# Placing the tiles that TensorE reads at multiples of 1024 bytes in a two-layer decoder trunk

## The reference

```python
def swiglu_ffn(x, norm_pre, w_gate, w_up, w_down, norm_post):
    h = rms_norm(x, norm_pre)
    a = jax.nn.silu(jnp.einsum('bsd,df->bsf', h, w_gate)) * jnp.einsum('bsd,df->bsf', h, w_up)
    y = jnp.einsum('bsf,fd->bsd', a, w_down)
    return x + rms_norm(y, norm_post)
def reference(x, ...):
    for layer in range(DEPTH):
        if layer % 2 == 0:
            x = ab_layer(x, ...)
        else:
            x = conformer_conv_layer(x, ...)
        x = swiglu_ffn(x, ...)
    return x
```

## The kernel before, in words

| tile | before | remainder | after | remainder |
|---|---|---|---|---|
| x | 16,512 | 128 | 18,432 | 0 |
| xT_hi, xT_lo | 32,896, 49,280 | 128 | 34,816, 51,200 | 0 |
| raw, w_hi, w_lo | 65,664, 82,048, 98,432 | 128 | 67,584, 83,968, 100,352 | 0 |
| gpost, tok | 114,816, 123,008 | 128 | 116,736, 124,928 | 0 |
| ident, ones | 133,856, 134,400 | 736, 256 | 17,120, 17,632 | 736, 224 |
| mix_hi, cT_hi, hT_hi | 136,160 | 992 | 136,192 | 0 |
| mix_lo, cT_lo; hT_lo | 152,544; 181,216 | 992 | 152,576; 181,248 | 0 |
| vd_hi, vd_lo, c_hi, c_lo | 177,120 to 209,888 | 992 | 177,152 to 209,920 | 0 |
| g_now, g_tail | 187,552, 189,856 | 160, 416 | 187,584, 189,888 | 192, 448 |
| sig, lin, sq, prod, conv_sum | 194,432 to 210,816 | 896 | 194,464 to 210,848 | 928 |
| diag, bias_rows, ones_r | 215,040, 217,088, 225,280 | 0 | 215,072, 217,120, 225,312 | 32 |

## Time and profile before

### The profile page before, as it was taken

The page is one execution under the profiler, slowest core; times in us unless marked ns, Lnnn a source line. Parts: engine busy times, 40 slices in busy tenths (PEclk is TensorE's granted clock), DMA queues, the critical chain, the costliest instruction groups (busy, mean ns, idle before and its releaser), DMA issues.

```text
span 2093.9 us, 28886 instructions
## 1 busy us (share of the span) xinstructions
PE 2056.2 (98%) x10074; PEld 1727.1 (82%) x10074; DVE 1181.5 (56%) x1449; ACT 986.2 (47%) x1165; POOL 197.5 (9%) x118
## 2 busy tenths in 40 slices
PE   8999999999999999999999989999999999999998
PEld 6798888888888888888899967788888888888886
DVE  5745465555555544444599996565555555544444
ACT  5544464545455443433744475454444444443433
POOL 0000000000000000000688640000000000000000
PEclk9999999999999999999999989999999999999999
DMA  7735465555555555555455415465555555555554
GB/s 240 246 129 187 171 211 192 185 189 188 190 189 190 188 185 188 187 186 190 130 190 184 156 61 171 161 220 189 189 190 188 190 189 190 188 184 190 185 187 141
DMA packets 105128, 382.31 MB, mean 183 GB/s; under 512 B 11682, under 2 KB 12066, under 8 KB 104546
## 3 DMA queue, kind: packets, MB, share of 16 engines
q1 hardware_dynamic: 103968, 375.58, 53.9%
q0 software_dynamic: 944, 5.51, 0.8%
q10 hardware_dynamic: 148, 0.27, 0.0%
HBM read 379.21 MB, written 2.10 MB: 182 GB/s over the span
## 4 chain that ended last, share of the span: by engine, by line
PE 86%; DVE 8%; issue 3%; DMA 1%; ACT 1%; DVEq 0%; POOL 0%; SPq 0%; ACTq 0%; POOLq 0%
PE acc L1158 80%; DVE acc L1065 5%; PE acc L1169 1%; PE acc L1171 1%; PE acc L1170 1%; PE acc L1350 1%; DMA raw<-in_units 1%; DVE taps_now L1046 1%; PE acc L1208 0%; PE acc L1210 0%; ACT w_hi L458 0%; DVE w_lo L780 0%; DMA vecs<-in_vecs 0%; ACT junk L468 0%; DVE conv L1067 0%
## 5 line engine op out<-in xcount | busy, mean ns | idle before, releaser
L780 DVE SCALAR_TENSOR_TENSOR w_lo<-raw,vecs,w_hi 128x1024 fp32r<-128x1024 f32 x400 | 512.6, 1284 | 476.3 <-ACT w_hi L458 474.6
L458 ACT ACTIVATE w_hi<-raw,vecs 128x1024 fp32r<-128x1024 f32 x400 | 459.2, 1151 | 527.8 <-PE acc L1158 492.2
L458 ACT ACTIVATE w_hi<-raw 128x1024 fp32r<-128x1024 f32 x304 | 322.1, 1062 | 481.0 <-PE acc L1158 378.8
L778 DVE TENSOR_TENSOR w_lo<-raw,w_hi 128x1024 fp32r<-128x1024 f32 x236 | 288.9, 1225 | 345.6 <-ACT w_hi L458 345.6
L1158 PE MATMUL acc<-w_hi,xT_hi 128*128 128x512 f32 x1536 | 477.8, 392 | 6.1 <-DVE w_lo L780 5.5
L1158 PE MATMUL acc<-w_lo,xT_hi 128*128 128x512 f32 x1536 | 473.6, 390 | 0.0
L1158 PE MATMUL acc<-w_hi,xT_lo 128*128 128x512 f32 x1536 | 473.4, 389 | 0.0
L1158 PEld LDWEIGHTS acc<-w_hi,xT_hi 128*128 128x128 f32 x1536 | 285.3, 188 | 68.1 <-DVE w_lo L780 6.3
L1158 PEld LDWEIGHTS acc<-w_lo,xT_hi 128*128 128x128 f32 x1536 | 288.6, 188 | 60.5
L1158 PEld LDWEIGHTS acc<-w_hi,xT_lo 128*128 128x128 f32 x1536 | 288.6, 188 | 60.3
L1158 PE MATMUL acc<-w_hi,hT_hi 128*128 128x512 f32 x704 | 222.8, 397 | 0.0
(11 more groups left out here) (155 smaller groups left out, 1510.6 us busy)
## 6 DMA issues: line engine op xcount, KB each, us to landing
raw<-in_units SPq DMA_DIRECT2D x708, 512.0 KB, 3.3
gpost<-in_post POOLq DMA_DIRECT2D x4, 1024.0 KB, 5.8
x<-in_x SPq DMA_DIRECT2D x4, 512.0 KB, 8.6
out<-x SPq DMA_DIRECT2D x8, 256.0 KB, 2.8
tok<-in_lng POOLq DMA_DIRECT2D x1, 512.0 KB, 7.0
tok<-in_lnb POOLq DMA_DIRECT2D x1, 512.0 KB, 9.8
bs<-in_bs POOLq DMA_DIRECT2D x1, 256.0 KB, 7.3
taps<-in_taps ACTq DMA_DIRECT2D x1, 248.0 KB, 2.6
```

The costliest lines, as they stand in the source:

```text
L458: nc.scalar.activation(out, raw[:, s, :], ACT.Copy, scale=scale).then_inc(hi_ready, 1)
L778: ins = nc.vector.tensor_tensor(out[:, s, :], raw[:, s, :], hi[:, s, :], ALU.subtract)
L780: ins = nc.vector.scalar_tensor_tensor(out[:, s, :], raw[:, s, :], vecs[:, gain:gain + 1], hi[:, s, :], ALU.mult, ALU.subtract)
```

## The change

The order of the allocations is changed and a start alignment is asked for. The small tiles (`vecs`, `ident`, `ones`, `warm`, the sums and variances) are allocated first, and the large common ones (`x`, `xT_hi`, `xT_lo`, `raw`, `w_hi`, `w_lo`, `gpost`, `tok`, `junk`, `rs_row`) behind them, each at a multiple of 1024 bytes. Of the stages' tiles, `mix_*`, `vm`, `vd_*`, `c_*`, `bs`, `cT_*`, `conv` and `hT_*` also get multiples of 1024. No instruction, wait, loop or DMA is added, removed or moved.

```diff
--- before.py
+++ after.py
@@ -40,6 +40,7 @@
 TAPS = 31
 PAD = TAPS - 1
 EPS = 1e-6
+ROW = 1024
 UNIT = 1024
 BANK = 512
 FFC = DFF // BANK
@@ -132,23 +133,14 @@
 def trunk(nc, d_x, d_units, d_vecs, d_taps, d_ident, d_bs, d_lng, d_lnb, d_bpw2, d_post, d_out):
     with ExitStack() as ctx:
         sb = lambda name, shape, dt=F32: ctx.enter_context(nc.sbuf_tensor(name, shape, dt))
+        row = lambda name, shape, dt=F32: ctx.enter_context(nc.sbuf_tensor(name, shape, dt, align_bytes=ROW))
         sem = lambda name: ctx.enter_context(nc.semaphore(name))
 
 
-        x = sb("x", [P, T, D])
-        xT_hi = sb("xT_hi", [P, KT, SEQ], F32R)
-        xT_lo = sb("xT_lo", [P, KT, SEQ], F32R)
-        raw = sb("raw", [P, 4, UNIT])
-        w_hi = sb("w_hi", [P, 4, UNIT], F32R)
-        w_lo = sb("w_lo", [P, 4, UNIT], F32R)
-        gpost = sb("gpost", [P, D])
-        tok = sb("tok", [P, D])
-        junk = sb("junk", [P, 2, BANK], mybir.dt.bfloat16)
         vecs = sb("vecs", [P, V_ALL])
         ident = sb("ident", [P, P])
+        ones = sb("ones", [P, P])
         warm = sb("warm", [P, 1])
-        ones = sb("ones", [P, P])
-        rs_row = sb("rs_row", [P, 1, SEQ])
         pow_exp = sb("pow_exp", [P, 1])
         y_sums = sb("y_sums", [P, T, 4])
         x_sums = sb("x_sums", [P, T, 4])
@@ -156,29 +148,41 @@
         x_var = sb("x_var", [P, T, 2])
         y_rs = sb("y_rs", [P, T])
         x_rs = sb("x_rs", [P, T])
+        x = row("x", [P, T, D])
+        xT_hi = row("xT_hi", [P, KT, SEQ], F32R)
+        xT_lo = row("xT_lo", [P, KT, SEQ], F32R)
+        raw = row("raw", [P, 4, UNIT])
+        w_hi = row("w_hi", [P, 4, UNIT], F32R)
+        w_lo = row("w_lo", [P, 4, UNIT], F32R)
+        gpost = row("gpost", [P, D])
+        tok = row("tok", [P, D])
+        junk = row("junk", [P, 2, BANK], mybir.dt.bfloat16)
+        rs_row = row("rs_row", [P, 1, SEQ])
         rs_diag = tok[:, 0:T * P].rearrange("p (t n) -> p t n", n=P)
         acc = ctx.enter_context(nc.psum_tensor("acc", [P, 8, BANK], F32))
 
 
         with ExitStack() as m:
             mb = lambda name, shape, dt=F32: m.enter_context(nc.sbuf_tensor(name, shape, dt))
-            mix_hi = mb("mix_hi", [P, KT, SEQ], F32R)
-            mix_lo = mb("mix_lo", [P, KT, SEQ], F32R)
-            vm = mb("vm", [P, D])
-            vd_hi = mb("vd_hi", [P, D], F32R)
-            vd_lo = mb("vd_lo", [P, D], F32R)
-            c_hi = mb("c_hi", [P, 4, UNIT], F32R)
-            c_lo = mb("c_lo", [P, 4, UNIT], F32R)
-            bs = mb("bs", [P, HEADS, P])
+            mrow = lambda name, shape, dt=F32: m.enter_context(nc.sbuf_tensor(name, shape, dt, align_bytes=ROW))
+            mix_hi = mrow("mix_hi", [P, KT, SEQ], F32R)
+            mix_lo = mrow("mix_lo", [P, KT, SEQ], F32R)
+            vm = mrow("vm", [P, D])
+            vd_hi = mrow("vd_hi", [P, D], F32R)
+            vd_lo = mrow("vd_lo", [P, D], F32R)
+            c_hi = mrow("c_hi", [P, 4, UNIT], F32R)
+            c_lo = mrow("c_lo", [P, 4, UNIT], F32R)
+            bs = mrow("bs", [P, HEADS, P])
             bn = mb("bn", [P, T, 12])
             mv = mb("mv", [P, T, 2])
             ln_var = mb("ln_var", [P, T])
             ln_rs = mb("ln_rs", [P, T])
         with ExitStack() as m:
             mb = lambda name, shape, dt=F32: m.enter_context(nc.sbuf_tensor(name, shape, dt))
-            cT_hi = mb("cT_hi", [P, KT, SEQ], F32R)
-            cT_lo = mb("cT_lo", [P, KT, SEQ], F32R)
-            conv = mb("conv", [P, KT, SEQ])
+            mrow = lambda name, shape, dt=F32: m.enter_context(nc.sbuf_tensor(name, shape, dt, align_bytes=ROW))
+            cT_hi = mrow("cT_hi", [P, KT, SEQ], F32R)
+            cT_lo = mrow("cT_lo", [P, KT, SEQ], F32R)
+            conv = mrow("conv", [P, KT, SEQ])
             taps = mb("taps", [P, KT, TAPS])
             taps_now = mb("taps_now", [P, 2, TAPS])
             g_now = mb("g_now", [P, 2, PAD + SEQ])
@@ -198,8 +202,9 @@
             ones_r = mb("ones_r", [2 * 32, P], F32R)
         with ExitStack() as m:
             mb = lambda name, shape, dt=F32: m.enter_context(nc.sbuf_tensor(name, shape, dt))
-            hT_hi = mb("hT_hi", [P, FT, SEQ], F32R)
-            hT_lo = mb("hT_lo", [P, FT, SEQ], F32R)
+            mrow = lambda name, shape, dt=F32: m.enter_context(nc.sbuf_tensor(name, shape, dt, align_bytes=ROW))
+            hT_hi = mrow("hT_hi", [P, FT, SEQ], F32R)
+            hT_lo = mrow("hT_lo", [P, FT, SEQ], F32R)
 
 
         raw_landed = [sem(f"raw_landed{s}") for s in range(4)]
```

## The result

| | before | after |
|---|---|---|
| median | 2096.50 us (4 runs, 2096.05 to 2096.64) | 2074.14 us (4 runs, 2073.36 to 2076.30) |
| span of the profiled execution | 2093.9 us | 2071.6 us |

The ratio is 0.9894, with a 95% interval of 0.9881 to 0.9906: the changed kernel is 22.4 us faster. The forecast was 2075.1 us.

A forecast was written before the change was run, and what follows sets the result against it. TensorE's matmul pace was taken to bound the kernel everywhere except the convolution. Part 1's 21.5 us, with parts 2 and 3 taken as 0, gave 2096.6 - 21.5 = 2075.1 us; range 2069 to 2099 us.

The forecast's parts named there:

- The bound: Whole chain: TensorE's own pace sets the time everywhere except the convolution, where VectorE's taps stand in the chain.
- part 1: Matmuls with hT, mix, cT stationary: starts at multiples of 1024 bring 234.3 to 226.8 ns, 2868 x 7.5 ns = 21.5 us.
- the half-clock matmuls behind the wait for cT_lo: Some 12 cT matmuls at 1.2 GHz, 427 ns each, show no placement cost and are left out of the gain.
- What distinguishes them: Allocation: xT's stationary blocks start at multiples of 64, those of hT, mix and cT at odd multiples of 32.
- Part 2: Moving x, xT, raw, w_hi, w_lo, gpost, tok from 128 to 0: bounds 0 and 13.5 ns per matmul, taken as 0.
- The add_bias rows: ones_r and bias_rows, both at 0: 278 ns each, fastest 385 ns; evidence against a 213 ns pace and that 0 is slow.
- Part 3: Small tiles' new starts: taken as 0 on VectorE and ScalarE, bounds plus or minus 1 us.
- The price of 0.9 us for prod: Convolution: 124 records moving prod through TensorE at 7.5 ns more each, covered by VectorE's taps, so taken as 0.
- (1): Slow pace comes from hT, mix, cT lying above byte 131,072, so it stays 234.3 ns; 2096.6 us, chance 0.26.
- the 16-byte lines of the Trainium skill: SBUF reads: penalty per crossing of 16-byte lines; starts at 992 and 0 cross equally many, so part 1 would give 0.
- (2): The constant 13.5 ns per 512-column matmul, beyond its columns' time, goes as well: 1969 us, chance 0.08.
- (3): xT at 0 gets hT's pace: 4608 x 7.5 = 34.6 us slower, 2131 us with hT unchanged; chance 0.04.

The follow-up runs named there:

- stage_only: Kernel before with a 32-byte tile behind x_rs: mix, cT, hT, c, vd move from 992 to 0, common tiles stay at 128; 2091.08 us, ratio 0.9976.
- stage_at_64: Changed kernel with the stages' tiles (mix, cT, hT, c, vd, conv) at 64 of their row, common tiles at 0; 2093.72 us, ratio 0.9989.
- one_pad: Kernel before with only a 160-byte tile behind x_rs: mix, cT and hT start at 128, as xT and w do; 2075.38 us, ratio 0.9902.
- xT_at_32: Changed kernel with xT_hi and xT_lo at 32 of their row, w, mix, cT and hT at 128; 2099.04 us, ratio 1.0018.
- w_at_32: Changed kernel with w_hi and w_lo at 32 of their row, xT at 0, mix, cT and hT at 128; 2120.55 us, ratio 1.0120.

## Why the prediction was right, and where it wasn't

**The bound.** TensorE's own pace was the bound and stayed it; its chain share rose from 86% to 88%, and ScalarE and VectorE served units at 2.72 us in the down projection too. No new wait came. Right.

**The size (part 1).** 7.5 ns times 2868 matmuls: the pieces show 7.4 to 7.6 ns, and 21.2 us against 21.5. The down projection's piece was to take 222.5 us for 981 matmuls; the chain now holds 1008 in one piece, and 981 at its 226.7 ns are 222.4. It was right to leave the half-clock matmuls behind the wait for cT_lo out of the gain: they stand 427 ns apart in both kernels. Their number was less sure. Before, the sixth pair behind the wait is the first short one (0.70 us), so ten and not 12 ran at the half clock; in the changed kernel it is the seventh (0.73 us, at 1245.08 us). Two matmuls more at the half clock cost 0.4 us, and so the first cT piece fell by 0.90 us and not by 180 x 7.5 ns = 1.35. In sum right; that the median came within 1 us of the forecast is in part luck, since the start ahead of the mix piece alone scatters by more.

**The reason (What distinguishes them, part 1).** The step that failed is "What distinguishes them". It named the start of the stationary block, a multiple of 64 or an odd multiple of 32. I looked at one side of the pair, because the other side, w at 128, is the same in every stage; that w stands at 128, as xT does, was in the table of starts, and I left it out of account. In its place the runs show the pair: 226.7 ns where both starts are equal modulo 256, whatever they are, and 232.4 to 234.3 ns at the seven other distances tried. `stage_only` and `stage_at_64` show the mistake with 2091.08 and 2093.72 us where that step wants 2074. The step gave the right time by luck, because the change sets both sides to 0. Had the change put hT at 64, the same reasoning would have foretold 2075 us, and missed.

**Part 2.** "0 for going from 128 to 0" was right as a sum, since xT and w keep their distance, but wrong as a statement on the change: with the stages' tiles at 0, the full gain of part 1 needs that move of w (`stage_only` without it: 5.2 us); the other way is to take the stages' tiles to 128 instead, as in `one_pad`. The add_bias rows, used as the proof that a start at 0 is good, have distance 0 on both sides before (217,088 and 225,280), and c_hi against vd_hi as well; they spoke for the pair, and I read them for the start.

**Part 3.** VectorE's and ScalarE's times hardly changed with the small tiles' starts. The mean record of a tap went from 482 and 480 to 487 ns, but the taps' pieces on the chain kept 22.7 us. The price of 0.9 us for prod didn't have to be covered, since it didn't fall due: TensorE's busy time for those 124 records went from 29.8 to 28.3 us. Right.

**The rivals.** (1), where the tiles lie, is refuted by the change and by `xT_at_32`. Its side argument was the 16-byte lines of the Trainium skill ("SBUF — State Buffer", Specifications). The runs don't bear it out as a rule for this effect: a distance of 32, a multiple of 16, costs 6.7 ns, and one of 4 costs 5.7. (2), the constant 13.5 ns: it remains, since no kernel here ran 512 columns at less than 226.7 ns. (3), a start at 0 that is bad for xT: refuted, but its cost, xT at hT's pace, is what `w_at_32` and `xT_at_32` brought about by the distance.

**Open.** What in TensorE makes the distance count isn't shown. That 0 and 256 are alike and 4 and 128 are not, that one pass in three disturbs the other two, and that nothing is lost at half clock, at 427 ns a matmul with the distance of 96 as with that of 0, would suit two streams of reads, the next block's and the moving columns', that settle into a rhythm or fail to; no run here looks inside, and this picture isn't shown.

## What to carry to other kernels

Where loads of 128x128 float32r blocks alternate with 512 moving columns, compare the pace (a piece of the chain over its count) between stages; if it differs by 2 to 3% at the same clock and shape, try the stationary and the moving tile at the same remainder modulo 256 bytes. It is the pair that counts: aligning one of them to any round number can leave the loss in place, and one pad of 160 bytes did here what moving every tile did. A change that gets its forecast time isn't thereby explained; undo its parts one by one before the reason is reused.

## What the runs showed of the hardware

- A 512-column float32r matmul behind its own block load runs at 226.7 ns if the two operands' starts are a multiple of 256 bytes apart, and at 232.4 to 234.3 ns at the distances 4, 32, 64, 96, 128, 160 and 224 modulo 256. At 256 columns the order is turned round, by about 1%: 120.0 ns at distance 0, 118.3 and 118.7 at 32 and 96.
- The Trainium skill ("TensorE: Matmul & The Clock Gate", "Part 2: What happens when you issue a matmul", the first step of "Step-by-step: what each phase is for") says that the next block's load reads through a port of its own and takes nothing from the running matmul's reads. Whether it is the reads that suffer, no run here shows; but a matmul of 512 columns behind its load isn't independent of where the loaded block lies, since it takes up to 7.6 ns more by the distance.
- A single pass in three at a distance of 32 slows the other two as well, 231.9 ns over the whole stream.
